# Gate and up of 20 of 22 feed-forward tiles by seven block products instead of eight, with x parked in memory meanwhile

## The reference

```python
def _swiglu(x, w_gate, w_up, w_down):
    return (jax.nn.silu(x @ w_gate) * (x @ w_up)) @ w_down
```

## Time and profile before

| what | value |
|---|---|
| median of 3 runs | 3095.77 us (3095.16 to 3097.09) |
| profiled execution, first to last instruction | 3092.8 us |
| PE busy | 3032.8 us, 98% |
| DVE busy | 1683.1 us, 54% |
| ACT busy | 1205.3 us, 39% |
| POOL busy | 288.2 us, 9% |
| matmuls at L1655 to L1657 | 3784 each |

### The profile page before, as it was taken

One profiled execution on the slowest core, in us unless ns is written; L12 is line 12 of the kernel. 1 busy time (PEld: TensorE's weight loads), 2 busy tenths in 40 slices (PEclk: granted clock), 3 DMA queues, 4 the chain that ended last, 5 costly groups with the idle time before them and its releaser, 6 DMA issues.

```text
span 3092.8 us, 40119 instructions
## 1 busy us (share of the span) xinstructions
PE 3032.8 (98%) x15272; PEld 2463.6 (80%) x15272; DVE 1683.1 (54%) x3050; ACT 1205.3 (39%) x2238; POOL 288.2 (9%) x344
## 2 busy tenths in 40 slices
PE   8999999999999999999999999999999999999998
PEld 7888887788888888778678888888778768888887
DVE  6653364446565426656756555436556766555434
ACT  4322334443432224644543322224545553322223
POOL 0000110001100012011001000013111001100002
PEclk9999999999999999999999999999999999999999
DMA  5333373225233233225125223334224315322332
GB/s 172 111 96 114 109 148 125 92 88 178 92 102 100 93 108 110 81 100 163 69 73 173 96 96 97 95 110 142 91 91 132 116 39 182 104 96 96 99 99 96
DMA packets 105999, 338.18 MB, mean 109 GB/s; under 512 B 15360, under 2 KB 15888, under 8 KB 105680
## 3 DMA queue, kind: packets, MB, share of 16 engines
q1 hardware_dynamic: 84816, 272.45, 27.4%
q0 software_dynamic: 20992, 63.15, 6.8%
HBM read 299.24 MB, written 27.52 MB: 106 GB/s over the span
## 4 chain that ended last, share of the span: by engine, by line
PE 90%; ACT 3%; DVE 3%; issue 2%; DMA 1%; POOL 0%; SPq 0%; POOLq 0%; DVEq 0%; ACTq 0%
PE bk L1655 26%; PE bk L1657 26%; PE bk L1656 26%; PE bk L1731 3%; PE bk L1753 2%; PE bk L1739 2%; ACT t L1893 1%; PE bk L1694 1%; PE bk L1695 1%; PE bk L1696 1%; DVE t L1974 1%; ACT t L1901 1%; ACT t L1841 0%; DVE t L2124 0%; PE bk L1707 0%
## 5 line engine op out<-in xcount | busy, mean ns | idle before, releaser
L1655 PE MATMUL bk<-t,t 128*128 128x512 f32 x3784 | 1483.5, 392 | 20.4 <-DVE t L1974 12.5
L1657 PE MATMUL bk<-t,t 128*128 128x512 f32 x3784 | 1469.7, 388 | 0.0
L1656 PE MATMUL bk<-t,t 128*128 128x512 f32 x3784 | 1468.1, 388 | 0.0
L1655 PEld LDWEIGHTS bk<-t,t 128*128 128x128 f32 x3784 | 712.8, 188 | 170.1 <-issue 19.7
L1657 PEld LDWEIGHTS bk<-t,t 128*128 128x128 f32 x3784 | 712.5, 188 | 147.0
L1656 PEld LDWEIGHTS bk<-t,t 128*128 128x128 f32 x3784 | 713.4, 189 | 141.6
L1974 DVE TENSOR_TENSOR t<-t,t 128x1024 fp32r<-128x1024 f32 (+3 forms) x538 | 615.6, 1163 | 370.2 <-ACT t L1841 369.7
L1841 ACT CAST t<-t 128x1024 fp32r<-128x1024 f32 (+3 forms) x538 | 513.6, 983 | 221.9 <-PE bk L1657 118.7
L1884 ACT CAST t<-t 128x512 fp32r<-128x512 f32 x88 | 54.7, 622 | 433.5 <-DVE t L2034 433.5
L1893 ACT ACTIVATE t<-t,t 128x256 f32<-128x256 f32 (+3 forms) x336 | 173.9, 519 | 123.0 <-DVE t L2047 122.4
L2280 POOL TENSOR_TENSOR t<-t,t 128x512 f32<-128x512 f32 x58 | 78.3, 1350 | 1387.0 <-ACT t L1871 1387.0
(11 more groups left out here) (173 smaller groups left out, 2008.7 us busy)
## 6 DMA issues: line engine op xcount, KB each, us to landing
t<-in_f_g SPq DMA_DIRECT2D x88, 512.0 KB, 4.3
t<-in_f_u SPq DMA_DIRECT2D x88, 512.0 KB, 3.5
t<-in_f_d SPq DMA_DIRECT2D x64, 512.0 KB, 4.4
t<-in_gate SPq DMA_DIRECT2D x48, 512.0 KB, 3.6
gate_scratch<-t POOLq DMA_DIRECT2D x64, 256.0 KB, 2.3
t<-gate_scratch POOLq DMA_DIRECT2D x64, 256.0 KB, 3.9
t<-in_f_d SPq DMA_DIRECT2D x32, 384.0 KB, 3.1
t<-in_wo SPq DMA_DIRECT2D x24, 512.0 KB, 3.7
```

Of the source, the lines that this page charges most:

```text
L1655: pe.matmul(o, wh, xh, start=start, stop=False)
L1656: pe.matmul(o, wh, xl, start=False, stop=False)
L1657: return pe.matmul(o, wl, xh, start=False, stop=stop)
```

## The change

For 20 of the 22 tiles in each of the four blocks gate and up are no longer two products of 128 x 1024 by 1024 x 512. The two tiles of weights (gate G over up U), each cut in two halves of the contraction (G1 G2, U1 U2, 4 chunks each), and h, cut in halves of the contraction and of the tokens, are a 2 x 2 by 2 x 2 block product. Strassen's scheme makes it of seven products instead of eight, each 4 chunks x 3 passes x 256 tokens, from sums of blocks:

- Weight sums, once per tile, on GpSimd: `total` 5 (U1+U2), 6 (that less G1), 3 (G2 less that), 7 (G1-U1).
- ACT casts and DVE subtracts for the halves of all seven left operands (128x512 each), where before it was two of 128x1024.
- Activation sums (`forms` 4 to 7) once per block, by `lift` (GpSimd, 16 subtractions of 128x256) and a split of each. They take the place of x (`xT`), which is parked in memory (`park_scratch`, from f2 on; f1 reads its input again) and fetched back behind the last pair tile.
- TensorE accumulates products 1, 6, 7 in bank A, 2 in B, 5 and 3 in C, 4 in D; ACT copies intermediate sums out (`snap` of 1, 6, 4, 5), DVE adds (`gate_low`, `gate_high`, `ups`), GpSimd multiplies (`scale` for up x `rstd`, `product` for gate x up).
- A `pair` step of tile U carries the tail of the tile before (Z) and the preparation of the next (V). The first two tiles stay plain and cover `lift` and `forms`. `abreast` in f2 falls from `wide=2` to `wide=1`; the rope tables are laid elsewhere; the hook in f1 runs in three steps of four.

```diff
     def ffn(...)
+        parked = [None if kept is None else self.load(kept[c], self.xT[:, c, :], xt[c]) for c in range(KC)]
...
+        for v, U in enumerate(us):
...
+            self.step("pair", U=U, V=us[v + 1] if v + 1 < len(us) else None, Z=us[v - 1] if v else None, load_to=U["u"] + 2)
...
+        xt = [self.load(self.xT[:, c, :], src[c], ("P", 6 + c // 4, last)) for c in range(KC)]
...
-        xs = self.ffn("f2", ht, wide=2)
+        xs, xt = self.ffn("f2", ht, xt, 4, xt, self.D["park"], wide=1)
```

TensorE:

```diff
+    def product(U, k, o, opens, lo, x):
+        u = U["u"]
+        e.wait_ge(("h", k, u), ("l", k, u), *U["x"][k])
+        for c in range(4):
...
+            pe.matmul(o, wh, xh, start=opens and c == 0, stop=False, skip_group_check=True)
+            pe.matmul(o, wh, xl, start=False, stop=False, skip_group_check=True)
+            ins = pe.matmul(o, wl, xh, start=False, stop=c == 3, skip_group_check=True)
+        e.then_inc(ins, "sums", ("P", k, u))
...
+            product(U, 1, A, True, ...)
+            product(U, 5, C, True, ...)
+            product(U, 2, B, True, ...)
+            e.wait_ge(("m", 1, u))
+            product(U, 6, A, False, ...)
+            product(U, 4, D, True, ...)
+            e.wait_ge(("m", 5, u))
+            product(U, 3, C, False, ...)
+            e.wait_ge(("m", 6, u))
+            product(U, 7, A, False, ...)
```

ACT, `pair` step:

```diff
+            if Z:
+                cast(U, 3)
+                bend(Z)
+            snap(U, 1)
+            if Z:
+                cast(U, 7)
+            snap(U, 5)
+            if V:
+                cast(V, 1)
+            if Z and V:
+                hidden(Z)
+            if V:
+                cast(V, 2)
+            snap(U, 6)
+            if V:
+                cast(V, 5)
+            snap(U, 4)
+            if V:
+                cast(V, 4)
+                cast(V, 6)
```

DVE:

```diff
+    def rest(U, k):
...
+        e.then_inc(dve.tensor_tensor(lo, src, hi, ALU.subtract), "rests", ("l", k, u))
+    def gate_high(U):
+        e.wait_ge(("P", 3, u), ("m", 6, u))
+        vec(dve.tensor_tensor(U["g"][:, 256:512], U["bank"][2], U["g"][:, 256:512], ALU.add), ("c12", u))
+        e.wait_ge(("c1", u), ("c12", u), U["r"])
+        vec(dve.tensor_tensor(U["g"][:], U["g"][:], P.rstd[:], ALU.mult), ("s", u))
+    def ups(U):
+        e.wait_ge(("P", 7, u), ("m", 4, u), ("m", 5, u))
...
+            if Z:
+                rest(U, 2)
+                ups(Z)
+                rest(U, 6)
+                rest(U, 3)
+                bent(Z)
+                rest(U, 7)
+            if V:
+                rest(V, 1)
+            gate_low(U)
+            if Z and V:
+                hidden(Z)
+            if V:
+                rest(V, 5)
+                rest(V, 4)
+            gate_high(U)
```

GpSimd (each of them one `tensor_tensor` of 128x512 from SBUF to SBUF):

```diff
+            if Z:
+                scale(Z)
+                total(U, 7)
+                product(Z)
+            if V:
+                total(V, 5)
+                total(V, 6)
+                total(V, 3)
```

More of the change, by code:

```diff
@@ L279, in dense, with abreast @@
         return b, bank, (n, "pe")
-    def abreast(self, names, xs):
+    def abreast(self, names, xs, ahead=2):
         got = [self.OB.take() for _ in names]
@@ L441, in postnorm @@
         store(1)
-        self.stream(4, on=("dve",))
+        self.stream(ahead, on=("dve",))
         k, spread = second()
@@ L501, in ffn @@
                 works += [(k, self.OB, *r[2 * k], *r[2 * k + 1]) for k in range(wide)]
-            gate_up(works, free + self.rope_done if hook is not None and j == 13 else free)
+            if j < plain - 1:
+                gate_up(works, free)
             if hook is not None:
                 next(hook, None)
-        return lambda c: (hid[:, 0, c, :], hid[:, 1, c, :], toks[c])
+        e0, e1, e2 = self.spl_free[0:3]
+        homes = {(0, 0): self.raw_free[0], (0, 1): self.raw_free[1], (1, 0): self.raw_free[2], (1, 1): e0}
@@ new lines, in ffn, with emptied @@
+        slots = {1: [e0, self.Sr.free[3], free], 5: [e0, e1], 6: e1, 2: e1, 4: e2, 3: e2, 7: e2}
+        us = [self.pair(name, j, (FC - 1 - j) % 2 ^ 1, slots, homes, None) for j in range(plain, FC)]
+        self.step("pair_in", U=us[0], load_to=us[0]["u"] + 1)
+        gate_up(works, free)
+        last = us[-1]["u"]
+        def emptied(U):
+            u = U["u"]
+            for (ring, b), t in zip(U["banks"], (("c2", u), ("c1", u), ("c12", u), ("m", 4, u))):
+                ring.give(b, t)
+            for i, t in zip(U["tmps"], ([("hh", u), ("hl", u)], [("prod", u)], [("z", u)])):
+                self.tmp.give(i, *t)
+            toks[U["j"]] = [("hh", u), ("hl", u)]
@@ new lines, in ffn @@
+        if hook is not None:
+            assert next(hook, None) is None
+        self.raw_free = [homes[0, 0], homes[0, 1], homes[1, 0]]
+        self.spl_free = [[("P", 5, last), homes[1, 1]], [("P", 6, last)], [("P", 7, last)], [("P", 5, last)]]
+        self.Sr.free[3] = [self.Sr.free[3], ("P", 1, last)]
+        self.ring, self.next_spl, self.next_raw = NSPL, 3, 0
+        self.stream(2)
+        self.step("pair_out", Z=us[-1])
+        emptied(us[-1])
+        src = [self.D["xT"][:, c, :] if kept is None else kept[c] for c in range(KC)]
```

320 lines of the change are left out of this document (282 added, 38 removed).

## The result

The kernel after takes 3439.11 us (median, 3438.58 to 3440.07); the kernel before, measured beside it, 3096.14 us (3095.16 to 3097.09). The ratio is 1.111, 95% interval 1.109 to 1.112: slower by 343 us. The forecast was 3355, range 3280 to 3450: the sign and the mechanism in the tiles held, the size was 86 us too small.

What follows compares the result with a forecast made beforehand. The prediction took TensorE, busy 98% of the span, as the bound before. Tiles +217, f1 start +3, f3 starts +4, f2 start +14, ends +8 and rope +12 made +258 on 3095.8: 3354, rounded to 3355 us, range 3280 to 3450.

Steps and rivals of the forecast that it cites:

- TensorE's part: Changed tiles: 84 narrow matmuls of 0.120 us take 10.08 us against 10.88, saving 64 us over 80 tiles.
- The shared path: Changed tiles: POOL tensor-tensor and VectorE two-SBUF-input operations exclude one another; 16 pass in turn, at least 12.3 us a tile.
- each engine's sum is under 10.08: Changed tiles: ACT 7.1, DVE 8.4, POOL 7.7 us alone; with free overlap a tile would take 10.08 us.
- The walk: One changed tile priced in program order: 12.3 us floor grows to a 13.8 us period, +217 us in all.
- The joints: Around the changed tiles: block starts f1 +3, f2 +14, f3 +2 each, ends +2 a block.
- The six: f2's start: with `wide` 1 instead of 2, the wide tile ends at 826.4 instead of 820.3, +6 us.
- the eight: f2's start: a split waits behind `forms`, POOL and the parking of the last x, +8 us (0 to 12).
- 20.6 fit barely: Block starts: POOL's 20.6 us of subtractions, sums and parking transfers fit beside two plain tiles of 21.8 us.
- The rope tables: f1: their 17 us of DVE work, formerly in DVE's idle time, cost +12 us (5 to 20).
- rival 3: Whole kernel: the clock falls to half pace, a tile takes 19.0 us, 3785 us in all; chance 0.03.
- Rival 1: Changed tiles: DVE and POOL overlap in most meetings, TensorE stays the bound, tile 10.08, 3061 us; chance 0.07.
- Rival 2: Changed tiles: POOL keeps the path through several operations, the chain becomes serial, 16.9 us a tile, 3622 us; chance 0.10.

Runs made afterwards that it cites:

- no_tail: all_dve with the two instructions up x rstd and product with gate left out, so hidden activations aren't right: 3139.2 us, 1.013 to 1.016 of before.
- psum_rest: Kernel after, with weight remainders in f2 and f3 reading one operand from idle PSUM columns instead of SBUF, values not right; f1 unchanged: 3283.7 us.
- tail_dve: Kernel after, with the last two POOL instructions of a pair tile (up x rstd, product with gate) run on VectorE: 3340.8 us.
- all_dve: Kernel after, with all six POOL instructions of a pair tile (four weight totals, up x rstd, product with gate) run on VectorE: 3224.5 us.
- pool_one: Kernel after, with POOL's totals for products 5, 6 and 3 replaced by one-input copies, so these sums are left out: 3284.8 us.
- lifts_dve: all_dve with the 64 subtractions that lift the token halves also moved from POOL to VectorE: 3213.5 us.
- early: Kernel after, with the step that builds the bias tables moved from f1's first tiles to the program's start: 3424.5 us.
- plain12: Kernel after, with the first 12 tiles of each block computed the old way instead of 2, and 10 by pairs: 3281.9 us.

## Why the prediction was right, and where it was short

**TensorE's part.** 119.9 ns a matmul and 10.08 us a tile: no_tail shows 119.6 and 10.05. Right.

**The shared path.** Right, and shown from three sides: take one operand off SBUF (psum_rest), take POOL off the path (tail_dve, all_dve), shorten what POOL does (pool_one). The price of a waiting VectorE operation, its end 0.54 us after POOL's, is 0.55 in after. The rest of the argument, "each engine's sum is under 10.08", was not the right test, as the prediction said; VectorE's own sum of 8.4 us is only what it would do alone.

**Floor and period.** The walk said 13.8 (13.3 to 14.7), the trace 13.92. The same walk with changed owners gave 12.4 (measured 12.40), 11.25 (11.27) and 10.9 to 11.3 (11.05). 12.3 us of contended operations were rightly not taken for the period. Of the predicted gaps, those ahead of products 5 and 2 are there and belong to remainders. Product 7's is there too, but with ScalarE's bank copy as the releaser, and product 3 has one I had not foreseen: ScalarE, which I had left as an engine with slack of a third, passes POOL's lateness on through its queue. POOL is at 68%, not over 85%: it idles 3.56 us a tile ahead of `scale`. Cost of the 20 tiles: 57 to 59 us a block in f2 and f3 against 54; with f1 taken as f2, 231 against 217, so 14 in all.

**The joints** are the term that was mis-sized most in f2 and f3. Their ends came as predicted, 1.9 to 2.0 us a block for 2. Their starts didn't. f1: 10.6 against 3, of which 6.74 are the wait for the wide tile's split and 2.4 the fallen clock behind it. f2: 20 against 14. The six (4.5 in seven waits of the wide tile) and the eight (8.70) for the split are there; not in the sum were 4.23 ahead of the first product and 1.2 that the fallen clock costs behind the 8.70. f3: 2 and 2 were predicted, 14 and 14 measured, of which in the first block 4.79 and 6.52 are idle time and 2.4 the fallen clock:
```profile
1941.98 0.80 PE L1776 MATMUL bk<-t,t 128*128 128x512 f32 x1 [4.79 <-DVE t L2299]
1956.77 0.55 PE L1787 MATMUL bk<-t,t 128*128 128x256 f32 x1 [6.52 <-DVE t L2221]
1964.90 0.39 PE L1787 MATMUL bk<-t,t 128*128 128x256 f32 x1 [1.72 <-ACT t L2012]
```
The step that failed is "20.6 fit barely". I added up POOL's work beside 21.8 us of TensorE's and left out that it comes in a chain with ScalarE and VectorE, that VectorE's `forms` stand behind it (and the activation's first operation behind `forms`, 4.79), and that the same exclusion stretches them. (The sum itself is 20.8 with the terms given, and a lift took 0.79 at the median, not 0.7.) The whole joint of f3, 16.0 in after, is 15.1 in all_dve and 12.0 in lifts_dve, where POOL has no arithmetic left there. So the path is 4 us of it at most, and the rest is order, latency and clock. In all 67 against 29 predicted.

**f1's queue** was missing altogether: 20 us of TensorE idle, because three instructions of POOL's queue that cost nothing beside an idle engine stood ahead of `total` 5. The prediction named POOL's idleness in the kernel before, and the parking transfers it is moved past, but not this chain. early and plain12 show it from two sides, and all_dve from a third.

**The rope tables** cost 17 us (the 11 tiles that they touch take 170.2 us for 153.1), predicted 12, range 5 to 20.

**The clock** was rival 3, for the whole kernel, and wrong there: 0.98 on average, full in the steady tiles, with TensorE at 79% by its records (72% by its matmuls' starts). But it fell where I had not looked: at the start of each block, after the idle stretches. At the lower level the narrow matmuls start 0.213 us apart. f1's stage has 319.8 us; 276 would be as f2, 20.0 are the wait, 17.1 the rope table, and 6 are left. The gap ahead of product 6 is 5.46 us, in f2's first changed tile 1.48: that is 4 of them. In f1's start 43 narrow matmuls run at the slow pitch (4.0 us), in f2's 27 (2.5 us): that is 1.5 more. The clock also fell in five of f1's rope tiles (92 matmuls at the slow pitch, 8.6 us of TensorE's time, each time behind 2.4 to 3.6 us of idle time); how much of that is in the 17.1, no run tells.

**Sum of the errors:** tiles 14, joints 38, f1's queue 20, rope 5, clock and gap 6, others 3: the 86 us.

**The range** held partly by luck. Its upper end took 60 us for everything besides the tiles; that measured 113 (67 of joints, 20 of f1's queue, 17 of rope, 6 and 3). The room came from the tile's upper bound, 14.7 us or 290 in all, where 231 were measured.

**Rival 1** would have been right only if most meetings had been free; none was. **Rival 2** (serial chain, 16.9 us a tile) isn't seen in the steady tiles. f1's tiles with a rope step do take up to 16.9 us (from one `scale` to the next 16.9, 15.2, 13.9, 16.9 and so on), but that is their added work: in all_dve, with POOL's six gone, the same tiles take 14.1, 12.4, 11.3, 14.1, so again up to 2.8 more than a plain one.

**Is any version faster than before?** Not among these. The best whole one, lifts_dve, is at 3213.5 us, 1.037 to 1.040 of before. Its tile of 11.27 is longer than the wide tile's 10.88. If VectorE were relieved of 1.2 us more per tile, no_tail shows what would be left: still 1.013 to 1.016.

## What to carry to other kernels

When work moves to an idle engine, don't add up each engine's time on its own: mark for each instruction which memory its inputs come from, and price GpSimd's SBUF instructions and VectorE's two-SBUF-input instructions as one lane. A busy share near 100% may be waiting; the mean of one form, beside the same form where nobody competes, tells which. And read the whole queue of an engine that was idle before: its waits were free, and they stop being free the moment something needed stands behind them. Last, an idle stretch of TensorE can cost more than its length: look at the pitch of the matmuls behind it.

## What the runs showed of the hardware that I had not expected

- VectorE got faster by being given more: 103 instructions more in 17 tiles, 42.7 us less recorded time (all_dve).
- An operation of VectorE that waits for POOL is recorded as running, from its start and not from its grant: 1.26 us on average for 0.69 of work.
- A GpSimd copy of 128x512 (fp32, SBUF to SBUF) takes 0.61 us alone, less than half of the 1.27 of a two-input sum of the same size, and it excludes VectorE all the same.
- The granted clock fell to the lower level after TensorE's idle stretches at the start of every block (4.2 to 20 us), and in f1 also behind some of 2.4 to 3.6 us; it was 0.63 in a row of 5 us in which TensorE was busy throughout, and the next row was full. At the lower level matmuls of 256 columns start 0.213 us apart instead of 0.120, those of 512 columns 0.427 instead of 0.227. In the steady tiles, with a gap of 0.4 to 1.2 us four times a tile, the clock stayed full.
